# Two FFN/mixer blocks, 1 core: another order of a mixer's weight units, dense rounds dealt by steps and carried convolution taps, one more low part on VectorE

## The chip, the cores and the metric

The kernel runs on one core of one Trainium2 chip. The metric is the device time of one execution in microseconds, and the changed kernel is compared with the one before on the same chip.

## The reference

A sequence of 256 tokens of width 1024 passes through two blocks of two layers each. All values are float32.

```python
...
def second_block(x, ...):                       # first_block: FFN, a mixer of four branches, FFN
    for i in range(DEPTH):
        x = layernorm(DN_ALPHA * x + 0.5 * swiglu_2(x, ffn_w13[i, 0], ffn_w2[i, 0]), ln_g[i, 0], ln_b[i, 0])
        y = hybrid_mixer(x, w_in[i], conv_w[i], ...)
        x = layernorm(DN_ALPHA * x + y, ln_g[i, 1], ln_b[i, 1])
        x = layernorm(DN_ALPHA * x + 0.5 * swiglu_2(x, ffn_w13[i, 1], ffn_w2[i, 1]), ln_g[i, 2], ln_b[i, 2])
    return x

def hybrid_mixer(x, w_in, conv_w, a_log, dt_bias, dn_norm_g, sink, w_branch_a, w_branch_b, w_out, pos_bias):
    qa, ka, va, qkv_b, beta_raw, dt_raw, z, gate_raw = jnp.split(x @ w_in, SPLIT_POINTS, axis=-1)
    ya = sliding_window_attention(qa, ka, va, pos_bias, sink) @ w_branch_a      # 16 heads, 4 kv heads of 64
    qkv_b = jax.nn.silu(causal_depthwise_conv_2(qkv_b, conv_w))                 # 4 taps, 3072 channels
    qb, kb, vb = jnp.split(qkv_b, (QK_B, 2 * QK_B), axis=-1)                     # 8 heads of 128
    qb, kb = l2norm(qb), l2norm(kb)
    beta = jax.nn.sigmoid(beta_raw); g = -jnp.exp(a_log) * jax.nn.softplus(dt_raw + dt_bias)
    o = gated_delta_rule(qb, kb, vb, g, beta)     # chunks of 64: a triangular solve per head, then a scan
    o = o * lax.rsqrt(mean(o * o) + NORM_EPS) * dn_norm_g * jax.nn.silu(z)
    yb = o @ w_branch_b
    gate_a, gate_b = jnp.split(jax.nn.sigmoid(gate_raw), 2, axis=-1)
    return (gate_a * ya + gate_b * yb) @ w_out
...
```

## The kernel before

**Weights.** They stream from memory in units of 128x2048 numbers through a ring of four slots. ScalarE rounds a unit to its high part (L1833), and VectorE (L2173) or GpSimd (L1140, eight pieces of 128x256) makes the low part, the rest of it. TensorE multiplies activations, split in the same way, with three matmuls of 128x256 for one round: high by high, low by high, high by low. A unit has 16 rounds. `Plan.by` says which engine makes a low part: in the second block GpSimd makes those of the mixer's units ("w" and "gy"), unless an FFN unit stands among the units just before it in the stream.

**The order.** It is written out in Python: `plan_first` and `plan_second` append steps, and every engine's queue is emitted in the order of the steps. PSUM has eight banks: 0 to 3 for dense products, 4 and 5 for attention and the solve, 6 and 7 for the preparation of a pair of delta heads, 3 also for `ddc`, `dkk` and `dot`.

**Block 2's mixer.** A chain of small steps depends on itself through VectorE and ScalarE: `score`, `turn` and `value` for each of 16 attention heads, then for each pair hp of delta heads a preparation (`ddc` decay matrices, `dtr` and `dte` transposed queries and keys and their norms, `dtf` transposed back after scaling, `dkk` products of keys) and a solve (`dl0`, four rounds of `dla` and `dlb` for levels s1 to s4, `du1` to `du4`, `dsc`), with `dot` (the output) of the pair before in it, and the preparation of the next pair woven in. Between these steps `interleave` deals rounds of dense units, so that TensorE has work while it waits: queries (`query`, step pq), the convolved channels (`conv(hp, w)`, step pconv: three units per pair), the z units (`gated`, step pz) and the gate units (`gate(i, k)`, step gy). `interleave` gives every step a share of the rounds by the step's weight w:

```python
        passed += w
        upto = total * passed // weight
```

**Taps.** A conv unit leaves its product in a bank; the four taps of the convolution then run on VectorE (L2574 and L2575, the last read being L2582's signal that the bank is free, and L2589 the silu's product), nine queue entries per conv. They are carried in the list `later` and taken from it one per chain step, or two while more than four wait, and all at once for a bank when a dense unit needs that bank:

```python
                while any(bank == host.jobs[0].bank for _, bank, _ in later):
                    later.pop(0)[2]()
```

**Lines of the steps.** On TensorE: L1547 score, L1562 turn, L1700 dtr, L1712 and L1716 dtf, L1735 dkk, L1744 dl0, L1755 dla, L1765 and L1767 dlb, L1726 ddc, L1807 dot; L1427 query, conv and z units, L1651 to L1657 gate units. On VectorE: L2387 the scalars of a score, L2610 the scaling behind dtr, L2662 the masked copy behind dla. Block 1 has in `plan_first` a convolution of 31 taps on VectorE (L2316), cut into 62 half-steps `conv_b`, some placed behind the projections cq and ck, the rest woven into later steps.

Of the kernel before, what the change touches and what calls it, by code (L numbers as in the profile page):

```python
# [91 lines left out]
class Plan:  # L92
# [35 lines left out]
    def close(self):  # L128
# [6 lines left out]
        for i, key in enumerate(self.stream):  # L135
            after_ffn = any(k[0] in ("gu", "d") for k in self.stream[max(0, i - 3):i])
            self.by.append("pool" if key[0] in self.by_pool and not after_ffn else "vector")
            self.tick("low_by_" + self.by[-1], QUARTERS)
            self.tick("high_ready", QUARTERS)
            self.tick("slots_free", 1)  # L140
            self.tick(("slot", i % SLOTS), 16)
# [116 lines left out]

def interleave(pl, chain, dense, later=(), keep=False):

# [8 lines left out]
    given, passed, done, later, begin = 0, 0, 0, list(later), len(pl.steps)  # L269
    todo, host = list(dense), None  # L270
    for w, f in chain:
        if f is None:
            while later and later[0][0] == w:
                later.pop(0)[2]()
            continue
        f()
        for _ in range(2 if len(later) > 4 else 1):
            if later and free(later[0][0]):
                later.pop(0)[2]()
        passed += w  # L280
        upto = total * passed // weight
        while given < upto:
            if host is None:
                rounds, make = todo.pop(0)
                host, rest = make()
# [21 lines left out]
def plan_first():  # L307
    pl = Plan()
# [71 lines left out]
    for what in ("cq", "ck"):  # L380
        for p in range(2):
            pl.steps.append(project(what, p)[0])
            for _ in range(3):
                conv_b()
# [89 lines left out]
def plan_second():  # L474
# [158 lines left out]
    def dot(h):  # L633
# [9 lines left out]
    dense = [(16, lambda p=p: query(p)) for p in (2, 3)] + [(16, lambda w=w: conv(0, w)) for w in range(3)]  # L643
    dense += [(16, lambda p=p: gated(p)) for p in range(2)] + [(16, lambda w=w: conv(1, w)) for w in range(3)]
    dense += [(16, lambda: gate(0, 0, "lo3"))]
    later = interleave(pl, chain, dense, keep=True)

    pairs = NH_B // 2
    extra = [[(16, lambda: gate(0, 1, "lo3"))] + [(16, lambda w=w: conv(2, w)) for w in range(3)],
             [(16, lambda: gated(2))] + [(16, lambda w=w: conv(3, w)) for w in range(3)],  # L650
             [(16, lambda: gated(3))] + [(16, lambda k=k: gate(0, k, "lo3")) for k in range(2, 5)],
             [(16, lambda k=k: gate(0, k, "lo3")) for k in range(5, 8)]]
    for hp in range(pairs):
# [4 lines left out]
        if hp + 1 < pairs:  # L658
            todo = [(2, f) for f in prepare((2 * hp + 2, 2 * hp + 3), ((6, 7), (6, 7)))]
            todo.insert(2, (hp + 1, None))  # L660
            ends = chain[-2:]
            chain = chain[:-2]
            for n, item in enumerate(todo[:9]):
                chain.insert(9 + 3 * n, item)
            chain += todo[9:] + ends
        later = interleave(pl, chain, extra[hp], later, keep=hp + 1 < pairs)
    open_gates = [gate(1, k, "lo3")[0] for k in range(2)]
# [71 lines left out]
def build_kernel(nc, x, stream1, stream2, prms, feat1, feat2, con, onehot, rowmask, relb, toep, out):  # L739
    with ExitStack() as ctx:  # L740
# [278 lines left out]
        def named(key):  # L1019
            return PLANS[now.blk].named[key]  # L1020
# [810 lines left out]
        def _(act):  # L1831
# [165 lines left out]
            def gy(st):  # L1997
# [3 lines left out]
                n = st.j  # L2001
                if now.blk == 2 and n < 4:
                    ready = named(("pz", n)).jobs[0]
                    act.wait_ge(bank_taken[ready.bank], taken_at(ready))
# [47 lines left out]
            def pz(st):  # L2052
                job = st.jobs[0]
                act.wait_ge(bank_full[job.bank], full_at(job))
                if st.p >= 2:
                    ready = named(("gy", st.p - 2)).jobs[0]
                    act.wait_ge(bank_taken[ready.bank], taken_at(ready))
# [763 lines left out]
```

## Time and profile before

| | us |
|---|---|
| median of three runs | 3156.67 (3151.34 to 3166.7) |
| profiled execution, its own time | 3169.31 |
| its span in the trace | 3167.5 |
| TensorE busy | 3016.7 |
| VectorE busy | 1914.9 |
| ScalarE busy | 1351.7 |
| GpSimd busy | 531.6 |

The span is the time from the profile's first instruction to its last. Busy times are sums over the span and say nothing of where an engine was late. The profiled execution stands 12.6 us above the median of the runs. Times in the rows are counted from the start of the span; block 2's mixers run at about 1680 to 2125 and 2520 to 2960 us.

### The profile page before, as it was taken

How to read it: one execution, taken by the hardware profiler on the slowest of the kernel's cores; microseconds unless marked ns; L12 is line 12 of the kernel's file. 1: busy time of each engine (PE TensorE's matmuls, PEld its weight loads, DVE VectorE, ACT ScalarE, POOL GpSimd, SP SyncE). 2: the span in 40 equal slices, each digit the busy share in tenths (PEclk: the TensorE clock that was granted, in tenths of full speed). 3: DMA queues.
4: the chain of work that ended last, by engine and by line, in shares of the span. 5: the costliest groups of instructions: out<-in, count | busy, mean ns of one | idle time of the engine just before them, and what ended most of it. 6: DMA issues, size and time to landing. Idle time of an engine off the chain costs nothing.

```text
span 3167.5 us, 54774 instructions
## 1 busy us (share of the span) xinstructions
PE 3016.7 (95%) x22114; PEld 2848.9 (90%) x22114; DVE 1914.9 (60%) x3377; ACT 1351.7 (43%) x2289; POOL 531.6 (17%) x837
## 2 busy tenths in 40 slices
PE   8999999999999999999998988999999999889998
PEld 7999999998989999898997988989989888889897
DVE  5557876656556876656655566456565645754655
ACT  4344454434344454434334544434343354443432
POOL 1000000000000000000003554540000065446000
PEclk9999999999999999999998999999999999999999
DMA  6545444554554456554563322245545432123553
GB/s 224 185 173 173 137 144 169 192 181 181 185 186 171 141 165 190 187 181 175 198 213 107 107 73 75 81 173 184 197 177 213 168 118 94 68 69 135 175 199 132
DMA packets 72861, 498.66 MB, mean 157 GB/s; under 512 B 8320, under 2 KB 8496, under 8 KB 19872
## 3 DMA queue, kind: packets, MB, share of 16 engines
q1 hardware_dynamic: 67824, 471.95, 42.3%
q0 software_dynamic: 4512, 22.20, 2.3%
q8 instruction: 176, 2.88, 0.4%
q10 hardware_dynamic: 272, 0.99, 0.1%
q14 instruction: 77, 0.63, 0.1%
HBM read 490.92 MB, written 4.19 MB: 156 GB/s over the span
## 4 chain that ended last, share of the span: by engine, by line
issue 48%; PE 35%; DVE 9%; POOL 3%; ACT 2%; DVEq 1%; DMA 1%; POOLq 1%; ACTq 0%
PE psum L1260 11%; PE psum L1427 5%; PE psum L1369 4%; PE psum L1651 3%; POOL weights_low L1140 2%; PE psum L1309 2%; DVE weights_low L2173 1%; PE psum L1657 1%; DMA weight_ring<-stream 1%; PE psum L1755 1%; PE psum L1395 1%; DVE work L2575 1%; PE psum L1547 1%; PE psum L1654 1%; PE psum L1767 1%
## 5 line engine op out<-in xcount | busy, mean ns | idle before, releaser
L1833 ACT ACTIVATE weights_high<-weight_ring 128x2048 fp32r<-128x2048 f32 (+5 forms) x782 | 907.3, 1178 | 859.3 <-DMA weight_ring<-stream 859.1
L2173 DVE TENSOR_TENSOR weights_low<-weight_ring,weights_high 128x2048 fp32r<-128x2048 f32 (+4 forms) x538 | 891.1, 1661 | 628.4 <-ACT weights_high L1833 626.2
L1260 PE MATMUL psum<-normed_t_high,weights_high 128*128 128x256 f32 x2560 | 725.1, 283 | 0.0
L1260 PE MATMUL psum<-normed_t_high,weights_low 128*128 128x256 f32 x2560 | 723.9, 283 | 0.0
L1260 PE MATMUL psum<-normed_t_low,weights_high 128*128 128x256 f32 x2560 | 723.9, 283 | 0.0
L1260 PEld LDWEIGHTS psum<-normed_t_high,weights_high 128*128 128x128 f32 x2560 | 490.6, 192 | 3.6 <-issue 0.6
L1260 PEld LDWEIGHTS psum<-normed_t_low,weights_high 128*128 128x128 f32 x2560 | 490.6, 192 | 3.0
L1260 PEld LDWEIGHTS psum<-normed_t_high,weights_low 128*128 128x128 f32 x2560 | 490.7, 192 | 0.0
L1140 POOL TENSOR_TENSOR weights_low<-weight_ring,weights_high 128x256 fp32r<-128x256 f32 x560 | 410.4, 764 | 245.5 <-ACT weights_high L1833 245.5
L1427 PE MATMUL psum<-normed_t_high,weights_high 128*128 128x256 f32 x1248 | 390.5, 313 | 9.4 <-DVE weights_low L2173 6.3
L1427 PE MATMUL psum<-normed_t_low,weights_high 128*128 128x256 f32 x1248 | 359.3, 288 | 0.0
L1427 PE MATMUL psum<-normed_t_high,weights_low 128*128 128x256 f32 x1248 | 359.1, 288 | 0.0
L1369 PE MATMUL psum<-weights_high,work_parts 128*128 128x512 f32 x1088 | 341.7, 395 | 0.0
L1427 PEld LDWEIGHTS psum<-normed_t_high,weights_high 128*128 128x128 f32 x1248 | 245.8, 197 | 23.5 <-issue 12.2
L1651 PE MATMUL psum<-normed_t_high,weights_high 128*128 128x256 f32 x768 | 233.8, 304 | 24.1 <-DVEq L2582 13.1
L1427 PEld LDWEIGHTS psum<-normed_t_low,weights_high 128*128 128x128 f32 x1248 | 246.0, 197 | 1.0
L1427 PEld LDWEIGHTS psum<-normed_t_high,weights_low 128*128 128x128 f32 x1248 | 245.0, 196 | 0.0
L1369 PEld LDWEIGHTS psum<-weights_high,work_parts 128*128 128x128 f32 x1088 | 199.3, 188 | 43.6
L1651 PE MATMUL psum<-normed_t_low,weights_high 128*128 128x256 f32 x768 | 220.1, 287 | 0.0
L1651 PE MATMUL psum<-normed_t_high,weights_low 128*128 128x256 f32 x768 | 220.0, 286 | 0.0
L1369 PE MATMUL psum<-weights_low,work_parts 128*128 128x512 f32 x544 | 214.9, 395 | 0.0
L1833 ACT ACTIVATE work<-psum 128x256 f32<-128x256 f32 (+5 forms) x276 | 118.4, 432 | 170.9 <-PE psum L1755 70.9
(279 smaller groups left out, 4668.3 us busy)
## 6 DMA issues: line engine op xcount, KB each, us to landing
weight_ring<-stream SPq DMA_DIRECT2D x400, 1024.0 KB, 4.8
weight_ring<-stream SPq DMA_DIRECT2D x64, 768.0 KB, 4.2
feature_rows<-feat POOLq DMA_DIRECT2D x12, 1024.0 KB, 5.4
work<-toeplitz_rows POOLq DMA_DIRECT2D x8, 512.0 KB, 6.5
toeplitz_rows<-work POOLq DMA_DIRECT2D x16, 192.0 KB, 3.9
params<-prms POOLq DMA_DIRECT2D x5, 239.5 KB, 2.9
residual<-x SPq DMA_DIRECT2D x2, 512.0 KB, 5.9
out<-residual SPq DMA_DIRECT2D x4, 256.0 KB, 2.0
```

Of the source, the lines that this page charges most:

```text
L1140: ins = pool.tensor_tensor(LOW[at], RING[at], HIGH[at].bitcast(F32), ALU.subtract)
L1260: ins = pe.matmul(PS[:, bank, at:at + S], w[a][:, first + k, c * P:(c + 1) * P], src[b][:, k, :], start=(k, m) == (0, 0), stop=(k, m) == ( ...
L1309: ins = pe.matmul(PS[:, job.bank, t * S:(t + 1) * S], XT[low][:, k, t * P:(t + 1) * P], w[part][:, k, :], start=n == 0, stop=n == len(FIRS ...
L1369: ins = pe.matmul(PS[:, b, :], src[c][:, r, t * P:(t + 1) * P], w[a][:, r, n * HALF:(n + 1) * HALF], start=start and m == 0, stop=False, s ...
L1395: ins = pe.matmul(PS[:, b, :], src[c][:, r, t * P:(t + 1) * P], w[a][:, r, n * HALF:(n + 1) * HALF], start=False, stop=stop and (r, m) == ...
L1427: ins = pe.matmul(PS[:, job.bank, c * S:(c + 1) * S], w[i][:, k, c * P:(c + 1) * P], XT[j][:, k, :], start=(k, m) == (0, 0), stop=(k, m) = ...
L1547: ins = pe.matmul(dst, q[:, t * P:(t + 1) * P], k[:, 0:keys], start=True, stop=not extra, skip_group_check=True)
L1651: ins = pe.matmul(PS[:, job.bank, 0:S], w[p][:, r, 0:P], XT[q][:, r, :], start=(r, m) == (0, 0), stop=(r, m) == (KB - 1, 2), skip_group_ch ...
L1654: ins = pe.matmul(PS[:, job.bank, S:2 * S], w[p][:, r, 0:P], y[q][:, r - KB, :], start=(r, m) == (KB, 0), stop=(r, m) == (11, 2), skip_gro ...
L1657: ins = pe.matmul(PS[:, job.bank, S:2 * S], w[p][:, r - KB, P:2 * P], y[q][:, r - KB, :], start=(r, m) == (KB, 0), stop=(r, m) == (15, 2), ...
L1833: return act.activation(dst, src, ACT.Copy, scale=scale)
L2173: dve.tensor_tensor(some(LOW, i, q, n), some(RING, i, q, n), some(HIGH, i, q, n).bitcast(F32), ALU.subtract).then_inc(low_by_vector, n)
```

## The change

Five edits. (1) `after_ffn` looks at four units before a mixer unit instead of three, so one more low part per layer of block 2, that of the query unit for pq(p1), goes to VectorE. (2) `interleave` counts carried taps beside the weights: the taps already carried, and `brought`, those that the units of this chain will bring. Each popped tap counts 1. Steps that take taps so get more rounds, the others fewer, and the last step takes what is left. (3) `plan_first` puts five half-steps instead of three behind each of four projections. (4) `plan_second` changes the order of units: all four z units come ahead of pair 1's convolutions, pair 1's third convolution and both first gate units move behind, into the pairs' solves, and so do the others. (5) The preparation of the next pair is inserted from item 12 of the solve on, not from 9. The waits of the TH buffer (tanh of z and gate) follow the new order.

```diff
--- before.py
+++ after.py
@@ -133,7 +133,7 @@
         assert len(self.place) == self.units
         self.by = []
         for i, key in enumerate(self.stream):
-            after_ffn = any(k[0] in ("gu", "d") for k in self.stream[max(0, i - 3):i])
+            after_ffn = any(k[0] in ("gu", "d") for k in self.stream[max(0, i - 4):i])
             self.by.append("pool" if key[0] in self.by_pool and not after_ffn else "vector")
             self.tick("low_by_" + self.by[-1], QUARTERS)
             self.tick("high_ready", QUARTERS)
@@ -256,7 +256,8 @@
                 pl.step(kind, signals=signals, s=s, j=j, p=args["j"].index(j))
 
 
-def interleave(pl, chain, dense, later=(), keep=False):
+def interleave(pl, chain, dense, later=(), keep=False, brought=0):
 
 
 
@@ -267,18 +268,22 @@
 
     total, weight = sum(rounds for rounds, _ in dense), sum(w for w, f in chain if f is not None)
     given, passed, done, later, begin = 0, 0, 0, list(later), len(pl.steps)
-    todo, host = list(dense), None
-    for w, f in chain:
+    weight += len(later) + brought
+    todo, host, final = list(dense), None, [item for item in chain if item[1] is not None][-1]
+    for item in chain:
+        w, f = item
         if f is None:
             while later and later[0][0] == w:
                 later.pop(0)[2]()
+                passed += 1
             continue
         f()
         for _ in range(2 if len(later) > 4 else 1):
             if later and free(later[0][0]):
                 later.pop(0)[2]()
+                passed += 1
         passed += w
-        upto = total * passed // weight
+        upto = total if item is final else min(total, total * passed // weight)
         while given < upto:
             if host is None:
                 rounds, make = todo.pop(0)
@@ -380,7 +385,7 @@
     for what in ("cq", "ck"):
         for p in range(2):
             pl.steps.append(project(what, p)[0])
-            for _ in range(3):
+            for _ in range(5):
                 conv_b()
 
     def score(br, e):
@@ -641,14 +646,13 @@
     chain = steps + [(0, None), (3, first[2])] + last + [(2, f) for f in first[:2]]
     chain += [(3, f) for f in first[3:5]] + [(9, first[5])] + [(4, f) for f in first[6:]]
     dense = [(16, lambda p=p: query(p)) for p in (2, 3)] + [(16, lambda w=w: conv(0, w)) for w in range(3)]
-    dense += [(16, lambda p=p: gated(p)) for p in range(2)] + [(16, lambda w=w: conv(1, w)) for w in range(3)]
-    dense += [(16, lambda: gate(0, 0, "lo3"))]
-    later = interleave(pl, chain, dense, keep=True)
+    dense += [(16, lambda p=p: gated(p)) for p in range(4)] + [(16, lambda w=w: conv(1, w)) for w in range(2)]
+    later = interleave(pl, chain, dense, keep=True, brought=36)
 
     pairs = NH_B // 2
-    extra = [[(16, lambda: gate(0, 1, "lo3"))] + [(16, lambda w=w: conv(2, w)) for w in range(3)],
-             [(16, lambda: gated(2))] + [(16, lambda w=w: conv(3, w)) for w in range(3)],
-             [(16, lambda: gated(3))] + [(16, lambda k=k: gate(0, k, "lo3")) for k in range(2, 5)],
+    extra = [[(16, lambda: conv(1, 2)), (16, lambda: gate(0, 0, "lo3"))] + [(16, lambda w=w: conv(2, w)) for w in range(2)],
+             [(16, lambda: conv(2, 2)), (16, lambda: gate(0, 1, "lo3"))] + [(16, lambda w=w: conv(3, w)) for w in range(2)],
+             [(16, lambda: conv(3, 2))] + [(16, lambda k=k: gate(0, k, "lo3")) for k in range(2, 5)],
              [(16, lambda k=k: gate(0, k, "lo3")) for k in range(5, 8)]]
     for hp in range(pairs):
         chain = [(2, f) for f in solve((2 * hp, 2 * hp + 1))]
@@ -661,9 +665,9 @@
             ends = chain[-2:]
             chain = chain[:-2]
             for n, item in enumerate(todo[:9]):
-                chain.insert(9 + 3 * n, item)
+                chain.insert(12 + 3 * n, item)
             chain += todo[9:] + ends
-        later = interleave(pl, chain, extra[hp], later, keep=hp + 1 < pairs)
+        later = interleave(pl, chain, extra[hp], later, hp + 1 < pairs, (18, 18, 9, 0)[hp])
     open_gates = [gate(1, k, "lo3")[0] for k in range(2)]
     for n, host in enumerate(open_gates):
         pl.steps.append(Step("part", None, src=host, a=0, b=8))
@@ -1999,8 +2003,8 @@
                 job, k = st.jobs[0], st.k
                 act.wait_ge(bank_full[job.bank], full_at(job))
                 n = st.j
-                if now.blk == 2 and n < 4:
-                    ready = named(("pz", n)).jobs[0]
+                if now.blk == 2 and n < 2:
+                    ready = named(("pz", n + 2)).jobs[0]
                     act.wait_ge(bank_taken[ready.bank], taken_at(ready))
                 elif n >= 2:
                     ready = named(("gy", n - 2)).jobs[0]
@@ -2053,7 +2057,7 @@
                 job = st.jobs[0]
                 act.wait_ge(bank_full[job.bank], full_at(job))
                 if st.p >= 2:
-                    ready = named(("gy", st.p - 2)).jobs[0]
+                    ready = named(("pz", st.p - 2)).jobs[0]
                     act.wait_ge(bank_taken[ready.bank], taken_at(ready))
                 act.activation(TH[:, st.p % 2, :], PS[:, job.bank, :], ACT.Tanh, scale=0.5).then_inc(z_tanh_ready, 1)
```

On VectorE, at block 2's entry to the mixer (small scalars of the decay, then the affine part of the norm, L2486 in the kernel before), before:

```order
L2531 SCALAR_TENSOR_TENSOR small<-small 128x8 x2
L2534 TENSOR_SCALAR small<-small 128x16
L2486 TENSOR_TENSOR residual<-work,feature_rows 128x512
L2488 TENSOR_TENSOR residual<-residual,feature_rows 128x512
L2486 TENSOR_TENSOR residual<-work,feature_rows 128x512
```

and now, four lines of code further down:

```order
L2535 SCALAR_TENSOR_TENSOR small<-small 128x8 x2
L2538 TENSOR_SCALAR small<-small 128x16
L2177 TENSOR_TENSOR weights_low<-weight_ring,weights_high 128x2048
L2490 TENSOR_TENSOR residual<-work,feature_rows 128x512
L2492 TENSOR_TENSOR residual<-residual,feature_rows 128x512
```

A whole low part has moved in front of the affine part.

On TensorE, at the first gate unit (gate(0,0)), before: the last round of pair 1's third convolution, then the gate's first round, then dtf of head 1.

```order
L1427 MATMUL psum<-normed_t_high,weights_high 128x256
L1427 MATMUL psum<-normed_t_low,weights_high 128x256
L1427 MATMUL psum<-normed_t_high,weights_low 128x256
L1651 MATMUL psum<-normed_t_high,weights_high 128x256
L1651 MATMUL psum<-normed_t_low,weights_high 128x256
L1651 MATMUL psum<-normed_t_high,weights_low 128x256
L1712 MATMUL psum<-constants,work 128x128 x4
L1716 MATMUL psum<-constants,work 128x128 x3
```

and now, in the solve of heads 0 and 1 (L1769 and L1771 are dlb, L1431 the convolution, L1655 the gate):

```order
L1769 MATMUL psum<-work 128x128 x2
L1771 MATMUL psum<-work 128x128 x2
L1431 MATMUL psum<-normed_t_high,weights_high 128x256
L1431 MATMUL psum<-normed_t_low,weights_high 128x256
L1431 MATMUL psum<-normed_t_high,weights_low 128x256
L1769 MATMUL psum<-work 128x128 x2
L1771 MATMUL psum<-work 128x128 x2
L1655 MATMUL psum<-normed_t_high,weights_high 128x256
```

The gate has moved from the preparation of heads 0 and 1 into their solve. By the plan it took bank 2 before, that of pair 1's first convolution, whose taps were drained just ahead of it; now it takes bank 1, whose taps stand 12 rounds earlier in the order.

On VectorE, behind the scaling of head 1 (L2610), before, with taps (L2574, L2575) among the copies of dtf (L2627, L2628):

```order
L2610 TENSOR_SCALAR work<-psum,small 128x128 x4
L2610 TENSOR_SCALAR feature_rows<-psum,small 128x128 x2
L2575 SCALAR_TENSOR_TENSOR work<-psum,params,work 128x254
L2575 SCALAR_TENSOR_TENSOR work<-psum,params,work 128x253
L2627 COPY work<-psum 128x256
L2628 COPY work<-psum 128x128
L2574 TENSOR_SCALAR work<-psum,params 128x256
L2575 SCALAR_TENSOR_TENSOR work<-psum,params,work 128x255
L2575 SCALAR_TENSOR_TENSOR work<-psum,params,work 128x254
L2575 SCALAR_TENSOR_TENSOR work<-psum,params,work 128x253
L2589 SCALAR_TENSOR_TENSOR work<-work 128x512
```

and now the same place, without them (L2639 and L2644 follow dkk, L2558 is the z unit's product):

```order
L2614 TENSOR_SCALAR work<-psum,small 128x128 x4
L2614 TENSOR_SCALAR feature_rows<-psum,small 128x128 x2
L2558 SCALAR_TENSOR_TENSOR work<-work,psum 128x512
L2631 COPY work<-psum 128x256
L2632 COPY work<-psum 128x128
L2631 COPY work<-psum 128x256
L2632 COPY work<-psum 128x128
L2639 TENSOR_TENSOR work<-psum,work 128x512
L2644 TENSOR_TENSOR work<-work,constants 128x128 x2
L2639 TENSOR_TENSOR work<-psum,work 128x512
L2644 TENSOR_TENSOR work<-work,constants 128x128 x2
```

The 27 entries of pair 1's taps have moved behind them, one or two to a step of the solve (L2578 and L2579 now).

## Rows read from the trace of the kernel before

**Rows 1.** The page: span, and busy time, share and instructions of two engines.
```profile
span 3167.5 us, 54774 instructions
...
PE 3016.7 (95%) x22114; PEld 2848.9 (90%) x22114; DVE 1914.9 (60%) x3377; ACT 1351.7 (43%) x2289; POOL 531.6 (17%) x837
```

**Rows 2.** Waits of TensorE: total us, times, longest us.
```profile
PE psum L1651 <- DVEq L2582: 13.1, 4, 3.7
PE psum L1712 <- DVE feature_rows L2610: 9.9, 6, 2.0
PE psum L1755 <- DVE work L2662: 9.2, 4, 2.6
PE psum L1744 <- DVE work L2671: 8.7, 6, 1.6
...
PE psum L1807 <- DVE work L2678: 7.3, 6, 1.5
...
PE psum L1700 <- DVE feature_rows L2610: 6.9, 6, 1.3
PE psum L1427 <- DVE weights_low L2173: 6.3, 2, 3.2
...
PE psum L1427 <- POOL weights_low L1140: 3.1, 2, 1.6
```

**Rows 3.** Timeline of TensorE: start us, us, line, shape, count, [idle before].
```profile
1821.63 0.28 PE L1427 MATMUL psum<-normed_t_high,weights_high 128*128 128x256 f32 x1
...
1821.99 0.28 PE L1427 MATMUL psum<-normed_t_high,weights_high 128*128 128x256 f32 x1
...
1826.55 0.55 PE L1651 MATMUL psum<-normed_t_high,weights_high 128*128 128x256 f32 x1 [3.68 <-DVEq L2582]
...
1829.46 0.41 PE L1651 MATMUL psum<-normed_t_high,weights_high 128*128 128x256 f32 x1
...
1830.10 0.41 PE L1651 MATMUL psum<-normed_t_high,weights_high 128*128 128x256 f32 x1
...
1850.59 0.64 PE L1765 MATMUL psum<-work 128*128 128x128 f32 x4
...
1851.43 0.48 PE L1657 MATMUL psum<-work_parts,weights_high 128*128 128x256 f32 x2
```

**Rows 4.** Windows: length, busy of PE, PEld, DVE, ACT, POOL, granted clock, DMA.
```profile
1826.55:1832.20 5.65, 5.65 (x26) 5.65 (x27) 2.78 (x5) 1.43 (x3) 5.65 (x9) 0.50 0.58 188
1841.03:1845.80 4.77, 4.77 (x28) 4.77 (x29) 4.17 (x10) 1.83 (x5) 3.85 (x6) 0.65 0.61 220
2658.18:2661.60 3.42, 3.42 (x16) 3.42 (x17) 2.21 (x4) 1.44 (x3) 3.42 (x5) 0.51 0.50 170
2671.30:2675.30 4.00, 4.00 (x21) 4.00 (x22) 3.24 (x7) 1.75 (x4) 3.08 (x5) 0.57 0.59 211
```

**Rows 5.** Groups of VectorE, 1680 to 2125 us: count, busy us, mean ns, idle.
```profile
L2575 DVE SCALAR_TENSOR_TENSOR work<-psum,params,work 128x255 f32<-128x255 f32 (+2 forms) x72 | 34.7, 481 | 6.0 <-issue 0.4
L2662 DVE COPY_PREDICATED work<-constants,psum 128x256 f32<-128x256 uint8 x88 | 34.6, 442 | 36.4 <-issue 35.8
...
L2589 DVE SCALAR_TENSOR_TENSOR work<-work 128x512 f32<-128x512 f32 x12 | 8.8, 737 | 4.9 <-ACT work L2065 4.9
```

**Rows 6.** Timeline of GpSimd, VectorE and TensorE at the start of the attention.
```profile
1698.26 25.10 POOL L1140 TENSOR_TENSOR weights_low<-weight_ring,weights_high 128x256 fp32r<-128x256 f32 x32 [18.28 <-ACT weights_high L1833]
...
1713.79 0.29 DVE L2381 CUSTOM_DVE_ANT_0 work<-psum,work 128x128 f32<-128x128 f32 x1 [8.22 <-issue]
...
1714.51 8.88 DVE L2387 TENSOR_SCALAR small<-small 128x2 f32<-128x2 f32 x1
...
1724.46 0.90 PE L1562 MATMUL psum<-constants,work 128*128 128x128 f32 x3 [8.05 <-ACT work L1955]
```

**Rows 7.** Timeline of VectorE in block 1's first cq/ck projections.
```profile
268.22 2.29 DVE L2173 TENSOR_TENSOR weights_low<-weight_ring,weights_high 128x2048 fp32r<-128x2048 f32 x1 [0.99 <-ACT weights_high L1833]
270.43 2.61 DVE L2316 SCALAR_TENSOR_TENSOR work<-work 128x255 f32<-128x255 f32 x6
```

## Prediction

> **What bounds the kernel now.** I read the page first: TensorE is busy in 3016.7 of 3167.5 us, VectorE in 1914.9 [rows 1]. The change leaves every matmul in place and moves two low parts a block from GpSimd to VectorE, so only two things can change: TensorE's waits, and the stretches in which its clock is low. The table of TensorE's waits comes next [rows 2]. What the reader is to see there is who is waited for: nearly always VectorE, in block 2's mixers. Third, the timeline at the largest of these waits. A dense round takes 0.36 us from start to start (1821.63 to 1821.99), and 0.64 us behind the wait of 3.68 us (1829.46 to 1830.10) [rows 3]. The windows show why: the granted clock is 0.50 there, the lower of its two levels, 1.2 GHz [rows 4]. So a wait has two prices, its length and the slow work behind it.
>
> **The change, part by part.**
>
> *A, the low part of pq(p1).* TensorE waited for GpSimd's low part twice, 3.1 us in all [rows 2]. GpSimd's run begins at 1698.26, as the high part is there, with 25.10 / 32 = 0.78 us a piece [rows 6], so its eight pieces take 6.3 us; VectorE makes the whole in 2.29 us [rows 7], 4 us sooner, more than the 1.6 us that TensorE waited at most. Both waits go: -3.1. The 2.29 us delay the affine part, and the first scores' scalars queue behind that; VectorE idled for 8.22 us before the first score [rows 6], so I charge nothing (2.3 us a layer if that cover is gone). Attention steps that carry no taps get 2.0 rounds instead of 2.33, and I charge one round of 0.36 us at two places a layer, the first turn and dtr(h0), where a fixed chain on the other engines sets the end: +1.4. A is -1.7.
>
> *B, the first gates.* Gate(0,0) and gate(0,1) took banks whose taps had to be drained first: 13.1 us in four waits [rows 2]. In the new order the taps stand 12 rounds or more ahead of the gate, so these waits go. Low clock behind them: length times what is missing from the granted clock [rows 4], 5.65 x 0.50 + 4.77 x 0.35 + 3.42 x 0.49 + 4.0 x 0.43 = 7.9 us. Together -21.0. Against this, all of pair 1's taps now lie in the solve's levels s1 to s3. VectorE there: 24 tap instructions at 0.48 and 3 products at 0.74 [rows 5] make 13.7; the masked copies, 88 for eight heads at 0.442 us [rows 5], are 4.86 us a head, of which three quarters for two heads are 7.3; about 1 us of small ones: 22.0 us. TensorE: 27 rounds at 0.36 are 9.7; six dlb at 0.84 (1850.59 to 1851.43 [rows 3]) are 5.0; eight dl0 and dla at about half of that 3.4; two ddc 0.5: 18.6. VectorE has no taps between the scaling and dkk any more and so begins the stretch ahead, by an estimate of mine 0.7 us, the one product (0.74) that stood there: TensorE waits 2.7 us a layer, anew: +5.4. I take one stretch of low clock per layer behind these waits, 1.7 us as in the last two windows [rows 4]: +3.4. B is -12.2 (bounds -21 and -5: no new wait, or the full 3.4 us and a second stretch of low clock twice).
>
> *D, the pairs' preparations.* Dtr and dtf wait for the scaling on VectorE, 6.9 and 9.9 us, and dl0 for L2671, 8.7 us, in six pairs each [rows 2]. What they wait for is a chain through ScalarE, GpSimd and VectorE that no round hurries, so each round fewer between two steps adds 0.36 us [rows 3]. By the order, 2 to 3 rounds fewer stand ahead of the second dtr and 2 ahead of dtf: 4.5 x 0.36 = 1.6 us a pair; one tap instruction of 0.48 us [rows 5] less stands on VectorE in between: net +1.1, for three pairs +3.3 a layer. Dkk and dl0 lose one round each: +0.7 a pair, +2.2. The levels s1 and s2, with taps, get 13 rounds instead of 10: the waits of dot and dla (7.3 and 9.2 us, [rows 2]) shrink by 3 x 0.36 = 1.1 for two pairs: -2.2. D is +3.3 a layer, +6.6 in all (bounds -4 and +14: either the taps' relief on VectorE covers the lost rounds, or none is felt and late taps add 1 us a pair).
>
> *Block 1.* A unit of cq or ck takes TensorE 16 x 0.36 = 5.8 us; VectorE then has 2.29 of low part, 2.61 of six instructions of convolution, and idles 0.99 [rows 7]. With five half-steps it has 2.29 + 4.35 = 6.6 us, so it falls behind by 0.8 us a unit, and reaches the scores some 3 to 4 us late; the scores wait there for little (TensorE works two steps ahead), and I charge 1.0 a layer. Eight half-steps, 7 us, then lie no longer among the later steps, where TensorE waited 6.3 us for VectorE's low parts [rows 2]: I give back 2.5 a layer. Block 1 is -3.0 (bounds -6 and +8).
>
> The new waits of the TH buffer are for units that end long before: nothing, since a z unit's product is read 32 rounds ahead of its next user; without that cover a round or two. Ring and DMA see the same units in another order: nothing, as 64 rounds last longer than four units take to land.
>
> *Sum.* -1.7 - 12.2 + 6.6 - 3.0 = -10.3 us, against the profiled execution's 3169.31, of which 3167.5 are the span; what lies around it does not change. That is -0.33%, and on the median of the runs, 3156.67, it gives **3146 us**.
>
> *One row that I weigh against a rule.* At the start of layer 0's attention VectorE's smallest instruction, 128x2, took 8.88 us, while GpSimd worked through 32 pieces without a break for 25.10 us; it ended when they did, and TensorE waited 8.05 us for what came of it [rows 6]. The clock was low behind it too. The Trainium skill, "SBUF — State Buffer", section "Terms", says that VectorE and GpSimd share a pair of ports, that one holds it for a whole instruction and that the other blocks fully meanwhile. By that rule a block would last at most one piece, 25.10 / 32 = 0.78 us, and the sum would stay as it is; the row shows a block as long as eleven pieces, and by the row the change, which shortens the run to 24 pieces starting later, still leaves the first scores inside it. So whether such a stall falls, and in which layer, I take as chance, worth 8.05 us and about half as much of low clock, 12 us; it is also about the distance of the profiled execution from the median.
>
> **The rivals.**
>
> 1. *The cover is better than I think* (chance 0.20). VectorE's new lead over the tap stretches suffices, the new waits of B stay out, and D ends even: -1.7 - 21.0 + 0 - 3.0 = -25.7, 3131 us. For it: VectorE idled 36.4 us ahead of the masked copies [rows 5], so it was not behind in the solves as a whole. Against: 22.0 against 18.6 us in the first one.
> 2. *The taps make VectorE the bound of the solves, and it gets slower* (0.15). Each of six stretches (pairs 0 to 2, two layers) costs the full 3.4 us and 1.7 of low clock, 5.1 to 5.5 with taps that drag into the next dtr. Without the relief of 2.2 in D the sum is -1.7 - 21.0 + 11.0 - 3.0 = -14.7, plus six times this price; with 5.5 it is +18.3, 3175 us. It decides from 5.1 us a stretch. For it: every wait of the table ends with VectorE. Against: in pairs 1 and 2 the taps are spread over the next preparation too, and the same idle 36.4 us.
> 3. *The stall of the scores falls otherwise* (0.20, half each way): 12 us more or less, 3134 or 3158 us.
> 4. *The gates wait all the same* (0.05). If VectorE is so late that the bank of the taps is still held when the gate comes, B returns to half of its 21.0: near 3155 us.
>
> **How the numbers follow.** The forecast has 0.40. A measurement of this kernel tells from no change about 0.5%, 15.8 us: 3140.9 to 3172.5. The forecast, a few us from its lower edge, gives 0.05 of its 0.40 to faster and 0.02 to slower; rival 1 is faster, half of rival 3 too, 0.02 of rivals 3 and 4 slower, rival 2 slower. Faster 0.05 + 0.20 + 0.10 = 0.35; slower 0.02 + 0.15 + 0.02 = 0.19; same 0.46. The range begins below rival 1 and half of rival 3, with B and D at their good bounds (-1.7 - 21 - 4 - 6 = -33, 3124, and a stall less), and ends short of rival 2: 3118 to 3171; the forecast's own is 3133 to 3159.
>
> **What the profile of the changed kernel would show.** A: no wait of L1431 (now) for GpSimd's low part. B: no wait of a gate unit for VectorE's drain, but 2 to 3 us of waits at dla in the solve of heads 0 and 1, and granted clock 1.0 at the first two gates; if dla waits over 5 us there, rival 2 is under way. D: dtr and dtf wait nearer 2 us than 1.2 and 1.7, dot and dla less than before. Block 1: a first score's scalars later on VectorE by 3 to 4 us, and less than 6.3 us for low parts behind. The prediction is wrong if VectorE's lead at dl0(h0) differs much from 0.7 us, or if the clock falls at those places though the waits are gone.

## The result and the profile after

The changed kernel takes 3139.41 us (median of 9 runs, 3131.96 to 3146.3), the kernel before 3156.67 (9 runs, 3149.34 to 3172.74). The ratio is 0.9937, with a 95% interval of 0.9916 to 0.9958. That is 17 us, or 0.6%. The profiled execution takes 3140.98 us:

```profile
span 3139.2 us, 54768 instructions
...
PE 3003.2 (96%) x22114; PEld 2835.8 (90%) x22114; DVE 1922.9 (61%) x3367; ACT 1351.1 (43%) x2281; POOL 526.7 (17%) x821
```

The span is 28.3 us shorter than in [rows 1]: TensorE is busy 13.5 us less with the same 22114 matmuls, so that part is clock, and idles 14.8 us less. The 28.3 us are more than the 17 us of the medians, because the profile of the kernel before stands 12.6 us above its median and this one 1.6 us. The table of TensorE's waits (total us, times, longest) against [rows 2]; line numbers are four higher:

```profile
PE psum L1759 <- DVE work L2666: 14.5, 10, 2.8
PE psum L1716 <- DVE feature_rows L2614: 14.1, 8, 2.8
PE psum L1704 <- DVE feature_rows L2614: 11.2, 6, 2.0
PE psum L1431 <- DVE weights_low L2177: 9.1, 4, 2.4
PE psum L1748 <- DVE work L2675: 8.5, 6, 1.6
...
PE psum L1655 <- POOL weights_low L1144: 4.6, 4, 1.9
...
PE psum L1811 <- DVE work L2682: 2.9, 6, 0.7
...
PE psum L1769 <- ACT work L1837: 2.8, 4, 1.0
PE psum L1730 <- DVE work L2623: 2.6, 2, 1.3
...
PE psum L1566 <- ACT work L1959: 1.7, 2, 0.9
```

The gates' wait for VectorE's drain (L2582) is gone, and so is pq(p1)'s for GpSimd. Dtr (L1704) and dtf (L1716) wait longer, 11.2 and 14.1 us instead of 6.9 and 9.9; dot (L1811) less, 2.9 instead of 7.3; dla (L1759) more, 14.5 instead of 9.2; dlb (L1769) and ddc (L1730) wait anew, 2.8 and 2.6. Two windows from dtr(h0) to the next pair's dtr or so, with the first gates in them (columns as in [rows 4]):

```profile
1785.00:1848.00 63.00, 55.83 (x452) 54.05 (x453) 41.62 (x121) 30.15 (x86) 38.83 (x58) 1.00 0.29 101
2614.00:2678.50 64.50, 56.25 (x451) 54.04 (x451) 43.19 (x119) 29.99 (x86) 38.33 (x58) 1.00 0.28 99
```

The granted clock is 1.00 throughout, where [rows 4] have 0.50 to 0.65. And the start of layer 0's attention (timeline of GpSimd, VectorE and TensorE), which answers to [rows 6]:

```profile
1692.18 18.99 POOL L1144 TENSOR_TENSOR weights_low<-weight_ring,weights_high 128x256 fp32r<-128x256 f32 x24 [22.74 <-ACT weights_high L1837]
...
1701.93 0.31 DVE L2391 TENSOR_SCALAR small<-small 128x2 f32<-128x2 f32 x1
...
1703.33 0.28 DVE L2391 TENSOR_SCALAR small<-small 128x2 f32<-128x2 f32 x1
...
1707.20 3.99 DVE L2391 TENSOR_SCALAR small<-small 128x2 f32<-128x2 f32 x1
...
1704.33 0.55 PE L1566 MATMUL psum<-constants,work 128*128 128x128 f32 x3 [0.86 <-ACT work L1959]
```

GpSimd's run is 18.99 us long. The first two scores' scalars pass in 0.3 us. The third is held for 3.99 us, to 1711.19, and the run ends at 1711.17. TensorE's first turn waits 0.86 us instead of 8.05.

Where the time went by place, read from the first instruction of the transposes (L1282 or L1286) at each border, in us from the start of the span:

| border | before | after | difference gained in between |
|---|---|---|---|
| end of block 1's first mixer | 551.24 | 542.50 | 8.7 |
| end of block 1's second mixer | 1281.79 | 1271.22 | 1.8 |
| entry of block 2's first mixer | 1671.09 | 1660.53 | 0.0 |
| its end | 2125.68 | 2102.11 | 13.0 |
| end of block 2's second mixer | 2958.70 | 2930.34 | 4.8 |

The FFN stages between them gain nothing.

### The profile page after: what moved, and what is told of

Its sections match the earlier page's. It is cut to its first block, busy times and chain, and to the rows that moved or that the text cites. A ratio compares the mean times of both kernels' runs of the same rounds, so it can differ in the third digit from the quotient of the medians.

```text
span 3139.2 us, 54768 instructions
## 1 busy us (share of the span) xinstructions
PE 3003.2 (96%) x22114; PEld 2835.8 (90%) x22114; DVE 1922.9 (61%) x3367; ACT 1351.1 (43%) x2281; POOL 526.7 (17%) x821
## 4 chain that ended last, share of the span: by engine, by line
issue 47%; PE 35%; DVE 8%; POOL 3%; DVEq 2%; ACT 1%; DMA 1%; POOLq 1%; ACTq 0%
PE psum L1264 11%; PE psum L1431 5%; PE psum L1373 4%; PE psum L1655 4%; POOL weights_low L1144 2%; PE psum L1313 2%; PE psum L1658 1%; DVE weights_low L2177 1%; PE psum L1661 1%; DVE work L2579 1%; DMA weight_ring<-stream 1%; PE psum L1551 1%; PE psum L1399 1%; ACT weights_high L1837 1%; DVEq L2574 1%
## 5 line engine op out<-in xcount | busy, mean ns | idle before, releaser
L2177 DVE TENSOR_TENSOR weights_low<-weight_ring,weights_high 128x2048 fp32r<-128x2048 f32 (+5 forms) x528 | 902.2, 1715 | 611.9 <-ACT weights_high L1837 609.8
L1431 PE MATMUL psum<-normed_t_high,weights_high 128*128 128x256 f32 x1248 | 388.9, 312 | 9.1 <-DVE weights_low L2177 9.1
L1431 PE MATMUL psum<-normed_t_low,weights_high 128*128 128x256 f32 x1248 | 358.3, 287 | 0.0
L1431 PE MATMUL psum<-normed_t_high,weights_low 128*128 128x256 f32 x1248 | 357.7, 287 | 0.0
L1373 PE MATMUL psum<-weights_high,work_parts 128*128 128x512 f32 x1088 | 341.7, 395 | 0.0
L1431 PEld LDWEIGHTS psum<-normed_t_high,weights_high 128*128 128x128 f32 x1248 | 244.7, 196 | 22.8 <-issue 17.4
L1431 PEld LDWEIGHTS psum<-normed_t_low,weights_high 128*128 128x128 f32 x1248 | 245.1, 196 | 0.8
L1431 PEld LDWEIGHTS psum<-normed_t_high,weights_low 128*128 128x128 f32 x1248 | 243.6, 195 | 0.0
L1655 PE MATMUL psum<-normed_t_high,weights_high 128*128 128x256 f32 x768 | 230.7, 300 | 5.2 <-POOL weights_low L1144 4.6
L1655 PE MATMUL psum<-normed_t_low,weights_high 128*128 128x256 f32 x768 | 216.8, 282 | 0.0
L1655 PE MATMUL psum<-normed_t_high,weights_low 128*128 128x256 f32 x768 | 216.7, 282 | 0.0
L1399 PE MATMUL psum<-weights_high,work_parts 128*128 128x512 f32 x576 | 181.9, 397 | 0.0
```

The source lines that it names most:

```text
L1373: ins = pe.matmul(PS[:, b, :], src[c][:, r, t * P:(t + 1) * P], w[a][:, r, n * HALF:(n + 1) * HALF], start=start and m == 0, stop=False, s ...
L1399: ins = pe.matmul(PS[:, b, :], src[c][:, r, t * P:(t + 1) * P], w[a][:, r, n * HALF:(n + 1) * HALF], start=False, stop=stop and (r, m) == ...
L1431: ins = pe.matmul(PS[:, job.bank, c * S:(c + 1) * S], w[i][:, k, c * P:(c + 1) * P], XT[j][:, k, :], start=(k, m) == (0, 0), stop=(k, m) = ...
L1655: ins = pe.matmul(PS[:, job.bank, 0:S], w[p][:, r, 0:P], XT[q][:, r, :], start=(r, m) == (0, 0), stop=(r, m) == (KB - 1, 2), skip_group_ch ...
L2177: dve.tensor_tensor(some(LOW, i, q, n), some(RING, i, q, n), some(HIGH, i, q, n).bitcast(F32), ALU.subtract).then_inc(low_by_vector, n)
```

## The experiments

Two theories stood against each other: that block 1's early half-steps and luck with the stall of 8 us at the first turn [rows 6] explain the two traces, or that the order of the units does. The first four kernels take the edits apart, each timed with the kernel before on the same chip.

**Block 1's half-steps alone.** The kernel before with

```diff
-            for _ in range(3):
+            for _ in range(5):
                 conv_b()
```

> The kernel before with one edit alone: five half-steps of the 31-tap convolution behind each of the four projections of block 1 instead of three. Theory 1 (the early half-steps are a main source of the gain: by the landmarks of the two traces block 1's two mixers became 10.4 us shorter): about 8 to 11 us faster than before, ratio near 0.997, with no wait of TensorE for the layer norm of the convolution (L1612) and none over 1 us for the gate units' low parts in block 1. Theory 2 (the 10.4 us are where the low clock happened to fall in the two profiles, and the edit is worth the 3 us of the forecast): 2 to 4 us faster, ratio near 0.999.

Measured: 3152.18 us against 3157.93, ratio 0.9980, interval 0.9955 to 1.0004. That lies between the theories. The timeline of VectorE in the first projections:

```profile
269.66 4.35 DVE L2316 SCALAR_TENSOR_TENSOR work<-work 128x254 f32<-128x254 f32 x10
273.92 2.29 DVE L2173 TENSOR_TENSOR weights_low<-weight_ring,weights_high 128x2048 fp32r<-128x2048 f32 x1
276.30 4.32 DVE L2316 SCALAR_TENSOR_TENSOR work<-work 128x251 f32<-128x251 f32 x10
```

Ten instructions now take 4.35 us behind each low part, with no idle time between, and the wait at the layer norm (L1612) is gone. Entry of block 2's first mixer, in the profiles taken: the six kernels with three half-steps, the kernel before among them, reach it at 1665.5 to 1671.1 us (mean 1667.4), the seven with five at 1657.4 to 1662.7 (mean 1660.1). That is some 7 us, and the kernel before had the latest of its group, so a part of the 10.6 in the table above was the one profile.

**All but the half-steps.** The changed kernel with `range(3)` again.

> The changed kernel with three half-steps again, all else as changed. Theory 1: it gives back 8 to 11 us, so it is 6 to 9 us faster than before, ratio 0.997 to 0.998, and the waits for L2316's end in block 1 are back. Theory 2: it keeps nearly all, 13 to 16 us faster, ratio near 0.995.

Measured: 3144.10 us, ratio 0.9957, interval 0.9938 to 0.9977. It keeps 13.8 of 17.3 us by the medians, so the half-steps are worth 3 us here; by the two ratios they are worth 0.2%, 6 us. Theory 1 had too much, theory 2 too little.

**The fourth low part alone.**

```diff
-            after_ffn = any(k[0] in ("gu", "d") for k in self.stream[max(0, i - 3):i])
+            after_ffn = any(k[0] in ("gu", "d") for k in self.stream[max(0, i - 4):i])
```

> The kernel before with one edit alone: a fourth low part per layer of block 2 on VectorE. Theory 1 (the wait of pq(p1) goes, and GpSimd's unbroken run ends before it can hold up VectorE's scalars of the first scores): 3 us of waits less, and the stall of 8.05 us at the first turn, with its low clock worth 12 us, is gone from all runs; if half of the runs of before have that stall in a layer, 8 to 10 us faster and a narrower spread of runs. Theory 2 (the stall is chance and stays as likely): 3 us faster, ratio 0.999, same spread.

Measured: 3143.91 us (3140.68 to 3147.07), ratio 0.9956, interval 0.9934 to 0.9977: 14 us, and a spread of 6 us over 12 runs where the kernel before has 28 over 35. Its waits:

```profile
PE psum L1651 <- DVEq L2582: 14.2, 4, 4.2
...
PE psum L1562 <- ACT work L1955: 1.2, 2, 0.6
```

The gates still wait 14.2 us; what has gone is the wait of pq(p1), 3.1 us, and the stall at the first turn, now 0.6 us at most. This one line brings most of the gain. How much of it is the stall can be estimated from the profiles. Four of them have it in one layer of two, and there the layer's mixer, from the transposes (L1282 or L1286) at its entry to those at its end, takes 454.6, 449.7, 448.7 and 453.5 us; that of the other layer in the same profile takes 445.3, 441.9, 438.4 and 444.5. That is 7.8 to 10.3 us for a stall, on average 9.1 (without any stall two layers differ by up to 6.0). Of the ten layers profiled with four units in GpSimd's run four had it, which makes 0.8 stalls in an execution of two layers: by this estimate 7.3 us, and with the 3.1 us of pq(p1) 10.4 of the 14. The interval of the ratio means 7 to 21 us, so the estimate lies within it; what the rest is, if it is real, stays open.

**The order and the dealing alone.** The changed kernel with three half-steps and the window of three.

> The changed kernel with three half-steps and the window of three again: the new order of units, the rounds dealt by steps and taps together, and the later insertion remain. Theory 1 (the gates' waits of 13.1 us and their low clock go, but the preparations' waits give most of it back): 2 to 6 us faster than before, ratio near 0.999. Theory 2 (the order is the main source, and the forecast's term B was right in full with little given back): 12 us or more faster, ratio 0.996 or less.

Measured: 3156.62 us against 3157.93, ratio 0.9995, interval 0.9976 to 1.0015. The order, the weights of the taps and the later insertion together bring nothing that can be measured. The same holds with the window of four: all but the half-steps takes 3144.10 us, the fourth low part alone takes 3143.91. In the profile of this kernel, with the window of three, layer 0 has the stall (timeline of the three engines):

```profile
1694.22 25.07 POOL L1144 TENSOR_TENSOR weights_low<-weight_ring,weights_high 128x256 fp32r<-128x256 f32 x32 [18.53 <-ACT weights_high L1837]
...
1710.48 8.84 DVE L2391 TENSOR_SCALAR small<-small 128x2 f32<-128x2 f32 x1
...
1720.39 0.90 PE L1566 MATMUL psum<-constants,work 128*128 128x128 f32 x3 [8.37 <-ACT work L1959]
```

The scalars are held for 8.84 us, and they end with GpSimd's run.

**Is it the form of the instruction?** The held instruction is a tensor_scalar; its neighbours in the same score, two-operand forms that read PSUM, were not held. The next two kernels write it in another form:

```diff
-                    last = dve.tensor_scalar(NM[:, e % 4, :], MX[:, e % 4, :], SINK8[:, e:e + 1], -QK_SCALE,
-                                             ALU.max, ALU.mult)
+                    last = dve.scalar_tensor_tensor(out=NM[:, e % 4, :], in0=MX[:, e % 4, :], scalar=SINK8[:, e:e + 1],
+                                                    in1=NEGQK[:, :], op0=ALU.max, op1=ALU.mult)
```

> The kernel before; only the 128x2 instruction behind each score of the sliding attention (L2387) is written as a scalar_tensor_tensor with a constant operand instead of a tensor_scalar, same values. Its neighbours, two-operand instructions of the same score, were not held up while GpSimd ran. Theory 1 (what GpSimd's unbroken run holds up is this form of instruction, so the stall of 7 to 9 us at the first score of layer 0 is a matter of the form): no instruction of that line over 1.5 us, no wait of 6 to 8 us at the first turn, 9 to 13 us faster than before, ratio 0.996 to 0.997, as far as the fourth low part alone. Theory 2 (GpSimd's run holds up any small instruction that comes at that moment, and the gain of the fourth low part comes from the end of the run and the wait of pq(p1)): the stall stays, within 3 us of before.

> The changed kernel with the same other form of that instruction. In its trace the third score of both layers is still held up for 3.9 us, and TensorE waits 1.5 us behind it. Theory 1: both blocks go, 3 to 6 us faster than the changed kernel, so near 0.993 of before. Theory 2: nothing changes, 0.9945.

Measured: 3158.67 against 3160.32 us, ratio 0.9996, interval 0.9973 to 1.0019, and 3139.66 us, ratio 0.9938 (interval 0.9916 to 0.9960), the changed kernel's. Theory 1 falls. In the kernel before with the new form, the stall of the profiled execution stands in the other layer (timeline of GpSimd, VectorE and TensorE in layer 1):

```profile
2526.80 25.11 POOL L1140 TENSOR_TENSOR weights_low<-weight_ring,weights_high 128x256 fp32r<-128x256 f32 x32 [18.71 <-ACT weights_high L1833]
...
2543.07 8.86 DVE L2387 SCALAR_TENSOR_TENSOR small<-small 128x2 f32<-128x2 f32 x1
...
2553.01 0.90 PE L1562 MATMUL psum<-constants,work 128*128 128x128 f32 x3 [8.04 <-ACT work L1955]
```

The new form is held for 8.86 us, to 2551.93; GpSimd's run ends at 2551.91.

**The weights of the taps.** The changed kernel without

```diff
-    weight += len(later) + brought
...
-                passed += 1
```

> The changed kernel with rounds dealt by the steps' weights alone, as before, in the new order of units. Theory 1 (counting the taps moves as many waits as it takes away): within 3 us of the changed kernel, dtr and dtf wait less (nearer 1.2 and 1.7 us a time than 1.9) and dla and dot more. Theory 2 (the taps need the rounds as cover; without them VectorE's drains stand in front of the dense units): 6 us or more slower than the changed kernel.

Measured: 3130.19 us (3128.35 to 3135.2), ratio 0.9908, interval 0.9884 to 0.9932. It is 9 us faster than the changed kernel. Theory 1 had the waits right in the main and their price too low. The waits of TensorE (line numbers one higher than before):

```profile
PE psum L1756 <- DVE work L2663: 13.8, 10, 2.8
PE psum L1713 <- DVE feature_rows L2611: 9.1, 6, 2.0
...
PE psum L1745 <- DVE work L2672: 8.7, 6, 1.6
PE psum L1808 <- DVE work L2679: 7.3, 6, 1.5
...
PE psum L1701 <- DVE feature_rows L2611: 7.0, 6, 1.3
...
PE psum L1756 <- DVE work L2651: 2.8, 4, 0.7
```

Dtf (L1713) is back at 9.1 and dtr (L1701) at 7.0 us, 9.2 us less than in the changed kernel; dot (L1808) is back at 7.3; dla waits 13.8 and 2.8, which is 2.1 more than in the changed kernel. By the two profiles TensorE idles 129.0 us instead of 136.0 and is busy 2997.5 instead of 3003.2, which is clock: the mean granted clock is 0.992 here and 0.989 in the changed kernel. The gates do not wait for VectorE's drain here either, so the new order by itself is enough for that.

**A window of five.** `i - 5` in the changed kernel, so VectorE makes one more low part and GpSimd's run is two units long.

> The changed kernel with a window of five: a fifth low part per layer of block 2 on VectorE, so GpSimd's run is two units long and ends before the third score. Theory 1 (the run's overlap with the scores is what counts): the blocks of 3.9 us at the third score go too, 3 to 5 us faster than the changed kernel. Theory 2 (VectorE, with 2.3 us more ahead of the scores, is late now): as fast or slower, with TensorE waiting at the first scores or turns.

Measured: 3136.44 us (3132.81 to 3142.69), ratio 0.9928, interval 0.9903 to 0.9953. Its blocks are gone (timeline of GpSimd and VectorE; the third score is shown):

```profile
1699.18 12.18 POOL L1144 TENSOR_TENSOR weights_low<-weight_ring,weights_high 128x256 fp32r<-128x256 f32 x16 [27.61 <-ACT weights_high L1837]
...
1709.38 0.62 DVE L2391 TENSOR_SCALAR small<-small 128x2 f32<-128x2 f32 x1
```

The run is 12.18 us long and no scalars of a score take more than 0.7 us. The 3 us agree with theory 1 but are not clear of the runs' spread.

**Three variations of the kernel without the tap weights**: insertion at item 9 again, a window of five, and seven half-steps.

> The changed kernel with rounds dealt by the steps' weights alone, and the preparation of the next pair inserted from item 9 of the solve again. Theory 1 (the order of the units is what removed the gates' waits; the later insertion matters little): within 3 us of the kernel without the tap weights (3130), ratio near 0.991, no wait of a gate unit for VectorE's drain. Theory 2 (the later insertion gives VectorE the time for the taps): 4 us or more slower than that, with waits at dla or dtr up by as much.

> Rounds by the steps' weights alone and a window of five. Theory 1 (a shorter run of GpSimd takes the blocks of up to 4.4 us off the third score, as the run with a window of five showed): 2 to 4 us faster than the kernel without the tap weights, ratio near 0.990. Theory 2 (what is left of the blocks is hidden behind rounds): within 2 us.

> Rounds by the steps' weights alone and seven half-steps behind each of the four projections of block 1. Theory 1 (five half-steps fill VectorE: 2.29 + 4.35 us a unit of 5.8 us; with seven it has 8.4 us a unit, the low parts come late and TensorE waits some 2.6 us a unit): 8 to 20 us slower than the kernel without the tap weights, ratio 0.993 to 0.997. Theory 2 (VectorE's lag is absorbed by the two steps that TensorE works ahead): 2 to 5 us faster.

Measured: 3130.06 us (0.9899, interval 0.9876 to 0.9923), 3132.47 us (0.9904, 0.9882 to 0.9925) and 3143.21 us (0.9943, 0.9923 to 0.9963). The later insertion does nothing that can be measured in this kernel, theory 1; nor does the fifth low part once the rounds are dealt by steps alone, theory 2. Seven half-steps cost 13 us, as theory 1 said, but not at the low parts: TensorE waits for the scalars of a score (L2391) in block 1, 12.5 us in both layers together.

```profile
294.22 1.65 PE L1548 MATMUL psum<-work 128*128 128x128 f32 x4 [5.55 <-DVE small L2391]
...
1029.12 1.65 PE L1548 MATMUL psum<-work 128*128 128x128 f32 x4 [6.92 <-DVE small L2391]
```

**The order of the units alone**, in the kernel before.

> The kernel before with the new order of units alone (and the waits of the TH buffer that follow it): rounds by the steps' weights, insertion from item 9, three half-steps and a window of three as before. Theory 1 (the order takes away the gates' waits of 13.1 us and low clock of 7.9, and nothing gives it back): 8 to 14 us faster than before, ratio 0.9955 to 0.9975; the stall of the first scores is still there in one of the layers. Theory 2 (the order is worth little by itself, and the kernel without the tap weights owes its time to the other edits acting together): within 4 us of before.

Measured: 3154.69 us (3140.75 to 3164.93) against 3160.14, ratio 0.9987, interval 0.9967 to 1.0007. The sign fits theory 1, the size neither: inconclusive by the interval. No gate waits for VectorE's drain. From its waits:

```profile
PE psum L1428 <- POOL weights_low L1141: 3.1, 2, 1.5
...
PE psum L1563 <- ACT work L1956: 1.1, 2, 0.6
```

Its profile, 3139.0 us of span, happens to have no stall at the first turn (0.6 us at most), and is the fastest of its runs. That would fit runs with no stall, with one and with two, some 10 us apart; but only profiles show stalls, so for the timed runs this is argued, not shown. Two profiles speak against it: that of the kernel before has one stall and stands among its slowest runs, and that of the order and the dealing alone has one and is the third fastest of twelve.

**The version that beats both** is the changed kernel without the tap weights, with either insertion: 3130 us, 1% below the kernel before.

## Why the prediction was right or wrong

The time, 3139, lies in the range and in the forecast's own range, and faster was given 0.35 against 0.46 for the same. The sum was -10.3 us and the runs show -17. That it came so near is in part luck: two misses of opposite sign, some 12 us in A and 4 to 6 in B and D, stand against each other. The terms:

*A was mis-sized, and that is the step that failed.* "I take as chance" put the stall of 8.05 us outside the sum, because a shorter run "still leaves the first scores inside it". They are inside it, and the third is held; but the fourth low part alone brings 14 us, not 1.7. Five kernels were profiled with GpSimd's run four units long. Of their ten layers, four show the first score's scalars held, for 7.4 to 8.9 us. Seven kernels have three units, and of their fourteen layers none does; nine of them hold the third, for 2.8 to 4.4 us. The first score comes some 9 us before the end of the run with three units as with four, so the length left is not what makes the difference. What does, stays open: at 16.25 us into a run the same instruction was held or passed, at 9.8 us it always passed. Where such an instruction is held beyond one piece, nineteen times in all profiles together, it ends 0.01 to 0.03 us behind GpSimd's last piece.

The scalars are not alone in this. Near the end of each mixer of block 2 VectorE makes a low part, 2.29 us by itself, while GpSimd makes two units. In 23 of the 28 layers profiled it takes 6.0 to 8.3 us, and in 22 of these it ends 2.15 us behind GpSimd's last piece, about its own length, as if it had begun only then. Once, in the kernel before, it was let in between two pieces. The changed kernel, layer 0 (timeline of VectorE and GpSimd):

```profile
2058.12 7.96 DVE L2177 TENSOR_TENSOR weights_low<-weight_ring,weights_high 128x2048 fp32r<-128x2048 f32 x1 [1.01 <-ACT weights_high L1837]
...
2058.30 5.62 POOL L1144 TENSOR_TENSOR weights_low<-weight_ring,weights_high 128x256 fp32r<-128x256 f32 x8
```

TensorE does not wait for it. By the rule in the Trainium skill, "SBUF — State Buffer", "Terms", that one engine blocks the other for an instruction, none of these blocks would have lasted beyond a piece of 0.78 us. The measurement decides: the blocking is there, its length is not the rule's. That shared ports are the reason, no run here shows.

*B was right in its old waits.* The four waits of 13.1 us are gone and the clock there is 1.00. New waits in the solve of heads 0 and 1 were forecast at 2.7 us a layer, at dla. In layer 0 they are 0.46 and 0.91 at L1769 and 0.95 at L1759, 2.3 us, and in layer 1 3.1 us; but more than half of layer 0's is at dlb, for ScalarE. No low clock came behind them. B's bad bound, -5, does not follow from the terms given for it (-21 + 2 x 3.4 + 4 x 1.7 = -7.4); the forecast does not use it.

*D was right in sign and near in size*, +6.6 forecast: dtr and dtf wait 8.5 us more; dot 4.4 us less, as much as was forecast for dot and dla together, and dla 5.3 more, of which about half is B's. Ddc's new wait, 2.6 us, stood in no term. The run without the weights gives the price in time, 9 us. What the prediction did not draw from this is that D and the new order can be had apart. Rival 2, the solves bound by VectorE, did not come.

*B and D together* were forecast at -5.6, and the runs give next to nothing: -1.3 us alone, +0.2 beside the fourth low part. The traces of the last pair show why. In block 2 TensorE idles 83.9 us with the new order and the dealing, and 79.3 without (idle time from 1600 us on): 13.9 less at the gates, and more at dtr, dtf, dla, dlb, ddc and dkk.

*Block 1 was mis-sized*: -3.0 forecast, 3 to 6 us by the timed runs, some 7 by the profiles. As forecast, the first score's scalars come 2.6 to 3.9 us later. But the wait that the 2.5 us were to come from grew, 6.3 to 9.1 us: at the old place it fell only from 3.15 to 2.40 us a layer, and ahead of it one of 1.84 (layer 0) and one of 2.45 (layer 1) are new. What went are others, most of all those of the gate units, and that of the layer norm (2.8 us). The lines before and after:

```profile
PE psum L1651 <- DVE weights_low L2173: 4.1, 4, 1.7
...
PE psum L1612 <- DVE work L2316: 2.8, 2, 1.6
```

```profile
PE psum L1655 <- DVE weights_low L2177: 0.4, 2, 0.2
```

With seven half-steps the lag costs 5.6 and 6.9 us at a score, so the slack that the five used up was nearly all there was.

So the outcome is the forecast's signs for B and D, which cancel, and rival 3's good half, which I gave 0.10: no profile with three or two units on GpSimd has the stall. By the estimate above that half was worth 7.3 us, not 12.

## What to carry to other kernels

A wait that comes in one layer of two and wanders between kernels is not luck to be left outside a sum: look for what both occurrences share, here a long unbroken run of another engine, and price the edit that shortens it. When rounds are dealt over steps, give them to the steps that wait for a chain of other engines, not to those that carry side work (9 us here); time the order and the dealing apart. Filling an engine's idle time early pays until its lag reaches the next step that others wait for, and then costs at once.

## What the runs showed of the hardware

A VectorE instruction of 128x2, 0.23 us by itself, is held in one of two ways while GpSimd runs one 128x256 subtraction behind the other: for less than one piece of 0.78 us (it takes 0.2 to 0.9 us in all), or to within 0.03 us of the end of the whole run, 8.88 us in the longest case. Two forms of the instruction behave alike (8.88 and 8.86 us). A subtraction of 128x2048 on VectorE, 2.29 us by itself, took up to 8.25 us beside such a run, and in 22 of 28 layers ended 2.15 us behind it.
